# Four norm factors of a decoder layer: column sums with a matrix of ones instead of narrow sums, a diagonal and a spread

## The reference

```python
def rmsnorm(x, g):
    y = xf * lax.rsqrt(jnp.mean(xf * xf, axis=-1, keepdims=True) + EPS)
    return (y * g.astype(jnp.float32)).astype(x.dtype)

h = rmsnorm(x, g_mix_pre)                       # factor 0
p = h @ w_in                                    # pool | conv (3 parts) | u | v
...
v = rmsnorm(v, sgu_norm)                        # factor 1, 768 wide, inside the gating heads
...
x = x + rmsnorm(mix @ w_out, g_mix_post)        # factor 2
f = conv_ffn(rmsnorm(x, g_ffn_pre), ...)        # factor 3: up, conv, gelu * val, down
x = x + rmsnorm(f, g_ffn_post)                  # last norm, computed per token row
```

## Time and profile before

| | |
|---|---|
| median of 3 runs | 1357.12 us (1356.16 to 1357.23) |
| profiled execution | 1358.99 us, its span 1357.3 us |
| PE busy | 1332.5 us, 98% |
| PEld busy | 1320.5 us |
| DVE busy | 758.4 us, 56% |
| ACT busy | 502.1 us, 37% |
| POOL busy | 104.6 us, 8% |
| chain that ended last | PE 95%, SPq 2%, DVE 2% |

### The profile page before, as it was taken

How to read it: one execution, slowest core, us unless ns; L and a number is a source line. 1 busy time by engine, 2 the same in 40 slices (tenths; PEclk the granted TensorE clock), 3 DMA queues, 4 the chain that set the end, 5 groups by cost and what they waited for, 6 DMA issues and landing times.

```text
span 1357.3 us, 24741 instructions
## 1 busy us (share of the span) xinstructions
PE 1332.5 (98%) x9026; PEld 1320.5 (97%) x9026; DVE 758.4 (56%) x1175; ACT 502.1 (37%) x727; POOL 104.6 (8%) x215
## 2 busy tenths in 40 slices
PE   5999999999999999999999999999999999999997
PEld 4999999999999999999999999999999999999996
DVE  6446855544458755544655554555555445656445
ACT  4323333333455433332333333333333333333652
POOL 4542000000014000000000000000000000000000
PEclk9999999999999999999999999999999999999999
DMA  8654455555563545456545545645544565554453
GB/s 222 162 155 137 118 149 142 145 153 152 140 179 94 155 131 152 124 149 188 149 130 155 143 128 149 186 135 155 155 135 129 149 174 155 155 145 135 112 150 114
DMA packets 379010, 199.59 MB, mean 147 GB/s; under 512 B 3924, under 2 KB 374592, under 8 KB 378968
## 3 DMA queue, kind: packets, MB, share of 16 engines
q1 hardware_dynamic: 378896, 198.83, 53.1%
q0 software_dynamic: 80, 0.31, 0.1%
HBM read 195.68 MB, written 3.56 MB: 147 GB/s over the span
## 4 chain that ended last, share of the span: by engine, by line
PE 95%; SPq 2%; DVE 2%; DMA 0%; issue 0%; ACT 0%; DVEq 0%; ACTq 0%
PE mm L491 30%; PE mm L492 30%; PE mm L495 30%; SPq L341 1%; PE tb L495 1%; PE tb L491 1%; PE tb L492 1%; PE tb L767 1%; DVE y_tok L1617 1%; DMA sgu_bias<-in_sgu_b_dram 0%; DVE a_lo L1431 0%; DVE f L1421 0%; SPq L355 0%; DVE up_lo L1148 0%; SPq L393 0%
## 5 line engine op out<-in xcount | busy, mean ns | idle before, releaser
L491 PE MATMUL mm<-a_hi,w_hi 128*128 128x320 f32 x1872 | 581.7, 311 | 0.0
L495 PE MATMUL mm<-a_lo,w_hi 128*128 128x320 f32 x1872 | 579.1, 309 | 1.8 <-DVE a_lo L1209 1.8
L492 PE MATMUL mm<-a_hi,w_lo 128*128 128x320 f32 x1872 | 578.6, 309 | 0.0
L867 ACT ACTIVATE w_hi<-raw 128x1024 fp32r (+3 forms) x384 | 352.8, 967 | 451.3 <-PE mm L495 431.0
L1160 DVE TENSOR_TENSOR w_lo<-raw,w_hi 128x1024 fp32r<-128x1024 f32 (+1 forms) x380 | 414.9, 1133 | 127.0 <-ACT w_hi L867 126.8
L495 PEld LDWEIGHTS mm<-a_lo,w_hi 128*128 128x128 f32 x1872 | 351.5, 188 | 2.8 <-DVE a_lo L1209 2.7
L491 PEld LDWEIGHTS mm<-a_hi,w_hi 128*128 128x128 f32 x1872 | 351.6, 188 | 1.2
L492 PEld LDWEIGHTS mm<-a_hi,w_lo 128*128 128x128 f32 x1872 | 351.6, 188 | 0.3
L495 PE MATMUL mm<-m_lo,w_hi 128*128 128x320 f32 x884 | 273.2, 309 | 0.0
L491 PE MATMUL mm<-h_hi,w_hi 128*128 128x320 f32 x660 | 205.7, 312 | 0.0
L492 PE MATMUL mm<-h_hi,w_lo 128*128 128x320 f32 x660 | 203.9, 309 | 0.0
(11 more groups left out here) (262 smaller groups left out, 914.5 us busy)
## 6 DMA issues: line engine op xcount, KB each, us to landing
raw<-in_ffn_up_dram SPq DMA_DIRECT2D x88, 1024.0 KB, 5.7
raw<-in_ffn_down_dram SPq DMA_DIRECT2D x60, 704.0 KB, 4.8
raw<-in_w_in_dram SPq DMA_DIRECT2D x34, 1024.0 KB, 5.6
raw<-in_w_out_dram SPq DMA_DIRECT2D x16, 1024.0 KB, 5.9
x_tok<-in_x_prompt_dram SPq DMA_DIRECT2D x4, 512.0 KB, 7.6
raw<-in_ffn_down_dram SPq DMA_DIRECT2D x2, 1024.0 KB, 6.2
out_dram<-y_tok SPq DMA_DIRECT2D x8, 256.0 KB
raw<-in_ffn_down_dram SPq DMA_DIRECT2D x1, 768.0 KB, 4.5
```

The source lines that it names most:

```text
L491: pe.matmul(out, whi[:, s], hi, start=start, stop=False)
L492: pe.matmul(out, wlo[:, s], hi, start=False, stop=False)
L495: return pe.matmul(out, whi[:, s], tile(lo, k), start=False, stop=stop)
L867: act.activation(w_hi[:, d:d + half], src, ACT.Copy).then_inc(w_hi_done, 1)
```

## The change

The partition sum becomes one matmul with the 128x128 matrix of ones as stationary operand and acc as the moving one (128x320). Its result holds each token's sum in every partition. Mean, root, reciprocal and Newton step are then done on 128x320. The diagonal, the spread and the copy go away, and with them the semaphores `diag_done` and `spread`; `r_done` is now counted by VectorE for all four factors. The old diagonal lay over acc and sq; now the mean is written over acc and the Newton term over sq. For factor 2 the sum is written to two banks, so that ScalarE takes the root straight from the sum in `tb[3]` (scale 1/D, bias eps from a spare column) while VectorE makes the mean from `tb[5]`; the factor itself goes back into `tb[5]`. `root(2)` moves ahead of a weight split on ScalarE. The filler matmuls become 4 and 22. The last norm keeps its narrow sums (`row_sums`).

```diff
-    diag = sb("diag", [P, 3, P], where="acc")
+    eps = cols[:, 0, 3:4]
...
             def token_sums(n):
                 pe.wait_ge(summed, SUMMED[n])
-                if n:
-                    pe.wait_ge(r_done, n - (n > 2))
+                pe.wait_ge(r_done, n)
                 if n == 3:
                     pe.wait_ge(f_scaled, KD)
-                tiles = TT if n == 4 else [(0, P), (P, P), (T - P, P)]
-                bank = mm[1] if n == 4 else tb[5]
-                parts = [acc, sq] if n == 4 else [acc]
-                if n == 4:
-                    pe.wait_ge(squared, 2 * KD + WIDE)
-                for i, (t0, nt) in enumerate(tiles):
-                    for part in parts:
-                        last = pe.matmul(bank[0:nt, i:i + 1], part[:, t0:t0 + nt], ones[:, 0:1],
-                                         start=(part is acc), stop=(part is parts[-1]))
+                pe.matmul(tb[5][:, 0:T], ones[:, :], acc[:, :], start=True, stop=True).then_inc(total, 1)
+
+            def row_sums():
+                pe.wait_ge(summed, SUMMED[4])
+                pe.wait_ge(squared, 2 * KD + WIDE)
+                for i, (t0, nt) in enumerate(TT):
+                    for part in (acc, sq):
+                        last = pe.matmul(mm[1][0:nt, i:i + 1], part[:, t0:t0 + nt], ones[:, 0:1],
+                                         start=(part is acc), stop=(part is sq))
                 last.then_inc(total, 1)
             def out_sums(part):
...
-                for i, t0 in enumerate((0, P, T - P)):
-                    last = pe.matmul(tb[5][:, i:i + 1], part[:, t0:t0 + P], ones[:, 0:1],
-                                     start=(part is acc and i == 0), stop=(part is sq and i == 2))
+                first = pe.matmul(tb[3][:, 0:T], ones[:, :], part[:, :], start=(part is acc), stop=(part is sq))
+                last = pe.matmul(tb[5][:, 0:T], ones[:, :], part[:, :], start=(part is acc), stop=(part is sq))
                 if part is sq:
+                    first.then_inc(twin, 1)
                     last.then_inc(total, 1)
-            def spread_r(n):
-                pe.wait_ge(diag_done, n + 1)
-                pe.matmul(tb[5][:, 64:64 + P], ones[:, :], diag[:, 0, :], start=True, stop=True)
-                pe.matmul(tb[5][:, 64 + P:64 + SEQ], ones[:, :], diag[:, 1, :], start=True, stop=True)
-                pe.matmul(tb[5][:, 64 + SEQ:64 + T], ones[:, :], diag[:, 2, P - TS:P],
-                          start=True, stop=True).then_inc(spread, 1)
...
             stay_warm(4)
             out_sums(sq)
-            stay_warm(10)
-            spread_r(2)
-            stay_warm(9)
+            stay_warm(22)
...
             def root(n):
-                act.wait_ge(meaned, n + 1)
-                act.activation(cols[:, 1, 0:3], cols[:, 0, 0:3], ACT.Sqrt).then_inc(rooted, 1)
-            def keep_r(n):
-                act.wait_ge(spread, n + 1)
                 dst = r_x if n == 0 else r_v
-                act.activation(dst[:, :], tb[5][:, 64:64 + T], ACT.Copy).then_inc(r_done, 1)
+                if n == 2:
+                    act.wait_ge(twin, 1)
+                    ins = act.activation(dst[:, :], tb[3][:, 0:T], ACT.Sqrt, scale=1.0 / D, bias=eps)
+                else:
+                    act.wait_ge(meaned, n + 1)
+                    ins = act.activation(dst[:, :], acc[:, :], ACT.Sqrt)
+                ins.then_inc(rooted, 1)
...
             act.activation(sq[:, :], mm[1][:, 0:T], ACT.Square).then_inc(squared, 1)
+            root(2)
             split_half(C_FFN + 2, 0, up_w[0][0])
-            root(2)
...
             def stats(n, width):
-                v, root, r, t = (cols[:, x, 0:3] for x in range(4))
+                v, t, r = acc[:, :], sq[:, :], (r_x if n == 0 else r_v)[:, :]
                 dve.wait_ge(total, n + 1)
-                dve.tensor_scalar(v, tb[5][:, 0:3], 1.0 / width, EPS, ALU.mult, ALU.add).then_inc(meaned, 1)
+                dve.tensor_scalar(v, tb[5][:, 0:T], 1.0 / width, EPS, ALU.mult, ALU.add).then_inc(meaned, 1)
                 dve.wait_ge(rooted, n + 1)
-                step(dve.reciprocal(r, root))
+                step(dve.reciprocal(r, r))
                 step(dve.scalar_tensor_tensor(out=t, in0=r, scalar=-0.5, in1=r, op0=ALU.mult, op1=ALU.mult))
+                dve.wait_ge(meaned, n + 1)
                 step(dve.tensor_tensor(t, t, v, ALU.mult))
-                step(dve.scalar_tensor_tensor(out=r, in0=t, scalar=1.5, in1=r, op0=ALU.add, op1=ALU.mult))
-                dve.tensor_tensor(diag[:, :, :],
-                                  ident[:, :].rearrange("p (a c) -> p a c", a=1).to_broadcast([P, 3, P]),
-                                  r.rearrange("p (a c) -> p a c", c=1).to_broadcast([P, 3, P]),
-                                  ALU.mult).then_inc(diag_done, 1)
+                dve.scalar_tensor_tensor(out=tb[5][:, 0:T] if n == 2 else r, in0=t, scalar=1.5, in1=r,
+                                         op0=ALU.add, op1=ALU.mult).then_inc(r_done, 1)
...
             def scale_out(k):
-                dve.tensor_tensor(tile(f, k), tile(f, k), tb[5][:, 64:64 + T],
+                dve.tensor_tensor(tile(f, k), tile(f, k), tb[5][:, 0:T],
                                   ALU.mult).then_inc(f_scaled, 1)
...
+            pool.memset(eps, EPS)
```

More of the change, by code:

```diff
@@ L229, in hybrid_layer @@
         total = sem("total")
+        twin = sem("twin")
         meaned = sem("meaned")
         rooted = sem("rooted")
-        diag_done = sem("diag_done")
-        spread = sem("spread")
         r_done = sem("r_done")
@@ L626, in _ @@
             chunk(C_V // 2, 0, a_hi, a_lo, order)
-            chunk(C_V // 2, 1, a_hi, a_lo, order, beside={1: [lambda: spread_r(0)]})
+            chunk(C_V // 2, 1, a_hi, a_lo, order)
             with pe.Fori(C_V // 2 + 1, C_POOL // 2) as q:
@@ L668, in _ @@
             chunk(C_POOL // 2, 0, a_hi, a_lo, order, beside={12: [lambda: token_sums(1)]})
-            chunk(C_POOL // 2, 1, a_hi, a_lo, order, beside={2: [lambda: spread_r(1)]})
+            chunk(C_POOL // 2, 1, a_hi, a_lo, order)
             pe.wait_ge(v_normed, NSGU)
@@ L730, in _ @@
             chunk(q0 + 1, 1, a_hi, a_lo, order, bank=tb[3], w=up_w[1])
-            chunk(q0 + 2, 0, a_hi, a_lo, order, beside={1: [lambda: token_sums(3)], 8: [lambda: spread_r(3)]},
+            chunk(q0 + 2, 0, a_hi, a_lo, order, beside={1: [lambda: token_sums(3)]},
                   bank=tb[4], hurry=True)
@@ L837, in _ @@
                     pe.wait_ge(drained[1], q_end)
-                    token_sums(4)
+                    row_sums()
             for j in range(len(PIECES)):
@@ L910, in _ @@
             root(0)
-            keep_r(0)
             with act.Fori(C_V // 2, C_POOL // 2) as q:
@@ L936, in _ @@
             split_hi(q0 + 1, 0)
-            keep_r(1)
             split_hi(q0 + 1, 1)
@@ L1011, in _ @@
             root(3)
-            keep_r(3)
             act.preload_act_table(ACT.Gelu_apprx_tanh)
@@ L1384, in _ @@
             steps[0] += PER_HEAD * NCONV
-            dve.wait_ge(spread, 2)
             step(dve.memset(acc[:, :], 0.0))
@@ L1413, in _ @@
             dve.memset(zf[:, 0:CH], 0.0).then_inc(zf_free, 1)
-            dve.wait_ge(spread, 3)
+            dve.wait_ge(r_done, 3)
             dve.wait_ge(drained[0], C_FFN // 2)
@@ L1463, in _ @@
                 split_half(C_FFN + 5, h, w_hi, w_lo, KD * P)
-            dve.wait_ge(r_done, 3)
+            dve.wait_ge(r_done, 4)
             dve.wait_ge(used, 2 * q0 + 4)
@@ L1552, in split_wide @@
                                           his[:, d].bitcast(F32), ALU.subtract).then_inc(w_lo_done, 1)
-                dve.wait_ge(spread, 4)
                 step(dve.memset(acc[:, :], 0.0))
@@ L1699, in _ @@
                 pool.tensor_tensor(tile(uT, j), tile(uT, j), r_x[:, :], ALU.mult).then_inc(u_scaled, 1)
-            pool.wait_ge(spread, 1)
             for j in range(NSGU):
```

## The result

| | before | after |
|---|---|---|
| median, same chip | 1357.12 us (5 runs, 1356.16 to 1359.61) | 1363.12 us (5 runs, 1362.28 to 1366.34) |
| profiled execution | 1358.99 us, span 1357.3 | 1366.34 us, span 1364.6 |

The medians lie 6.0 us apart. The ratio is 1.0049, 95% interval 1.0036 to 1.0063, which is 4.9 to 8.5 us slower. A second set of five runs gave 1363.72 against 1357.92 us, ratio 1.0046 (1.0032 to 1.0059). The forecast was 1363.5 (1359.0 to 1366.8), slower.

What follows compares the result with a forecast made beforehand. The prediction took TensorE, busy 98% of the span, to bound the kernel. The four factors' terms, -0.78 + 1.26 + 3.24 + 2.65 = +6.4 us, took the median from 1357.1 to 1363.5 us, range 1359.0 to 1366.8.

Steps and rivals of the forecast that it cites:

- What bounds: Whole kernel: TensorE, busy 98% of the span with almost no waits after start-up; VectorE's slack at four places matters.
- TensorE's side: TensorE's own stream: 0.78 us less at factors 0, 1 and 3; +0.42 us at factor 2 for acc.
- The reciprocal: VectorE, all four factors: 2.08 us on 320 columns, carried from two narrow rows at 6 ns per further column.
- the other operations' rate: Same four chains: reciprocal no slower than other operations, 0.49 us; +1.6 us in all, 1358.7; chance 0.12.
- upper bound: VectorE's wide reciprocal at most 3.5 us, from a slope of 10.5 ns a column using the shortest one-column run.
- The chain: VectorE, from reciprocal's start to its next instruction: R + 1.60 us, R being the reciprocal's 2.08; before, 1.28 us.
- Factor 1: VectorE's last normalisation of v 2.37 us later against 1.16 us of slack; TensorE waits, net +1.26 us.
- Factor 2: TensorE has only filler, so VectorE's chain lies bare: +2.82 us, and +0.42 for acc, +3.24 us.
- the signs: Traces to confirm the forecast, including first chunk matmul behind factor 2's filler at 405 to 406, waits totalling about 3.4 after factor 3.
- Factor 3: VectorE 2.65 us late with no slack before the last early split; TensorE's 0.78 us bring nothing, net +2.65 us.
- Sum: Four factors together: -0.78 + 1.26 + 3.24 + 2.65 = +6.4 us, median from 1357.1 to 1363.5.
- Rival 3: Factor 2: TensorE's clock falls after 3.7 us or so of idle; at most +1.0 us, 1364.5; chance 0.17.

Runs made afterwards that it cites:

- the pieces: The changed kernel with each wide reciprocal cut into four, of 16, 48, 96 and 160 columns; one execution, 1367.76 us against 1356.46, time not used.
- factor 2 alone: The kernel before with only factor 2 in the new form; 1361.62 us against 1356.46 (ratio 1.0038).
- the last kernel: The kernel before with factors 0 and 1 in new form, and ScalarE's reciprocal-root guess for factors 1 to 3; 1354.93 us against 1357.92 (0.9984).

## Why the prediction was right, point by point

- *What bounds*: TensorE, with next to no waits, so the question was VectorE's slack at each factor. Right: every microsecond lost is a new wait of TensorE for a late VectorE, or the clock behind such a wait.
- *TensorE's side*: 0.54 us for the wide sum and 0.66 each for sums and spread. The distance at factor 0 is -0.80 for -0.78, acc at factor 2 +0.41 for +0.42.
- *The reciprocal*: 2.15 us for 2.08. It carried the whole forecast: at the other operations' rate the sum would have been +1.6. That two narrow rows were enough was partly luck: the slope of 6 ns rests on 12 ns between medians that vary by 3, and the same rows gave 10.5 ns as an upper bound. The cost is linear, as the pieces showed, and so it carried over to 320 columns. The Trainium skill's repeat count of 8 ("VectorE: DVE Perf Modes", section "First, the fixed hardware budget") points the right way, but 6.25 ns a column is six cycles of 0.96 GHz, and the measurement decides.
- *The chain*: from reciprocal to the next work 3.65 us for 3.68. Small errors cancel: the reciprocal was 0.07 us longer; the scalar_tensor_tensor with a constant took 0.49 us instead of the 0.55 that I had scaled from one with a column as its scalar; and the last pass held VectorE 0.41 us (123.87 to 124.28) instead of 0.47.
- *Factor 1*: slack of 1.16 us and a stall of 1.82 us, net +1.29 for +1.26. *Factor 2*: +3.27 for +3.24. That the first matmul came at 406.07, in the 405 to 406 of the signs or nearly, says nothing by itself, since an earlier start (-1.64) and the fall behind factor 1 (+1.57) happen to cancel in it. *Factor 3*: no slack, net +2.47 for +2.65. I expected 3.4 us of waits, the last of them on a split; it is 2.7 in sum, the first on a split and the last on a bank, and the last early split came on time.
- *Sum*: +6.2 us in the trace without the clock for +6.4, and +6.0 in the medians. With the clock the trace has +9.0 and its second execution +9.1, so that the medians agree so closely holds only for executions without most of the falls, and the sum had no term for them.
- *Rival 3*, the clock at factor 2, was given 0.17 and at most +1.0 us. It happened in both profiled executions of the changed kernel, at +1.23 and +0.82 (one low stretch also with factor 2 alone, +0.86). I bounded it by one low stretch of 3.4 us; in the first it was 6.9 us. The step that failed is that I looked only at the longest idle: the clock also fell behind 1.8 us of waiting at factor 1, which the sum puts at nothing, and there nothing hides it, +1.57 and +1.39 us. Filler ahead of these waits removed the falls. Here the Trainium skill ("TensorE: Matmul & The Clock Gate", section "What's actually happening") would have done better than I did with it: activity lifts a throttled default state, and the trace agrees, granted clock 0.50 behind the wait, though not behind every wait of that length.
- The profiled execution lost 2.8 us to the clock, and the median still is 6.0, not 9.0, above the kernel before. The median execution had a mean granted clock of 0.997, where the profiled one had 0.993 (the kernel before 0.998), so it most likely lacked these falls. The start-up moves single executions by up to 4.7 us more, and only profiled ones show where.

## What to carry to other kernels

Before a narrow calculation is widened to all partitions and columns to save a spread, price its dearest instruction per column: a pair of narrow rows of different width gives the slope, the more surely the further the widths are apart. Do it factor by factor, for the same edit was worth -0.8, +1.3, +3.3 and +2.5 us in four places, by the cover that each had. And when something is ready earlier, look at what it starts: here GpSimd's products met a split and cost TensorE 1.9 us, at a factor where the earlier result saved nothing.

## What the runs showed of the hardware

- VectorE's reciprocal on fp32 in SBUF: 153 ns + 6.25 ns a column (16 to 320 columns), against 0.49 us at 320 columns for the plain operations.
- ScalarE's absolute reciprocal square root takes the time of a root (0.47 us at 128x320). Beside Copy and Square it needed no further table load. Between it and Sqrt a load of 1.28 us stood each time (74.10 and 117.05 in the last kernel).
- VectorE and GpSimd on SBUF at the same time: a pair of halves that takes 2.36 us alone took 3.44 and 3.49 where its halves and GpSimd's instructions took turns (halves of 1.62 to 1.90 us, GpSimd's six products 7.08 and 7.04), and 7.18 and 7.70 where the products all went ahead (first half 5.52 and 6.04, products 5.07). In the second case it began 0.64 and 0.11 us after them, but it had also begun after them, by 1.13 us, in the kernel before, where they took turns.
- The granted clock fell to half (1.2 GHz, matmuls 0.267 us apart for 0.147) at 14 of the 16 waits of TensorE of 1.8 to 4.3 us behind the start-up in the traces of this study, with full streams before them, and at none of the three of 1.6 us. The same wait can have a fall in one execution and none in the next (factor 3 in the two traces of the changed kernel). The half stretches lasted 3.4 us, one 6.9. They began 0.2 to 1.4 us after TensorE had resumed, and that one 1.6 us before it did.
